# First token tile and mask constants moved from GpSimd's load queue to ScalarE's and SyncE's

## What is computed

```python
mod = silu(c) @ w_ada + b_ada                # 6 x 1024, split in shift1, scale1, gate1, shift2, scale2, gate2
h = rms_norm(x) * (1 + scale1) + shift1
q, f, i, g, B, C, hv = split(h @ w_in)       # 7 blocks of 512 columns
# HGRN2 recurrence over q, f, i with output gate g; short convolution over B, C, hv
x = x + gate1 * (concat[o_hgrn, o_conv] @ w_out)
x = x + gate2 * (relu(rms_norm2(x) @ w_up)**2 @ w_down)
y = rms_norm(x) * g_final
```

## Time and profile before

| what | value |
|---|---|
| three runs | 895.25, 898.47, 898.91 us |
| profiled execution, its own time | 894.26 us |
| its span, slowest core (core 0) | 892.7 us |
| spans of the eight cores | 883.8 to 892.7 us |
| PE busy | 825.2 us, 92% of the span |
| DVE, ACT, POOL busy | 482.7, 361.1, 173.4 us |
| GpSimd's queue (q0) | 44.14 MB written, 29.6% of the 16 DMA engines' time |
| SyncE's queue (q1), ScalarE's (q10) | 55.46 and 6.03 MB, 18.3% and 2.1% |

### The profile page before, as it was taken

The page is one execution under the profiler, slowest core; times in us unless marked ns, Lnnn a source line. Parts: engine busy times, 40 slices in busy tenths (PEclk is TensorE's granted clock), DMA queues, the critical chain, the costliest instruction groups (busy, mean ns, idle before and its releaser), DMA issues.

```text
span 892.7 us, 16990 instructions; the slowest of 8 cores (883.8 to 892.7 us)
## 1 busy us (share of the span) xinstructions
PE 825.2 (92%) x6005; PEld 521.0 (58%) x6005; DVE 482.7 (54%) x902; ACT 361.1 (40%) x771; POOL 173.4 (19%) x231
## 2 busy tenths in 40 slices
PE   1488899999999999876999999999999999999996
PEld 1356687677775776734544654465456545654864
DVE  1365797577777867771551764256335634542422
ACT  3266874546667666612401532233123312311412
POOL 3110134344115235200002101100210111011002
PEclk9888999999999999989999999999999999999999
DMA  8999914958995243999993513122222113102001
GB/s 154 193 193 195 200 45 98 193 171 173 205 206 139 96 142 72 189 167 173 187 210 109 194 52 115 48 95 71 95 84 71 60 48 118 36 13 89 30 2 48
DMA packets 27727, 106.71 MB, mean 120 GB/s; under 512 B 3798, under 2 KB 4822, under 8 KB 22652
## 3 DMA queue, kind: packets, MB, share of 16 engines
q0 software_dynamic: 6624, 44.14, 29.6%
q1 hardware_dynamic: 19292, 55.46, 18.3%
q10 hardware_dynamic: 1728, 6.03, 2.1%
HBM read 123.93 MB, written 22.68 MB: 164 GB/s over the span
## 4 chain that ended last, share of the span: by engine, by line
PE 81%; DMA 7%; issue 4%; DVE 4%; ACT 3%; POOL 0%; DVEq 0%; ACTq 0%; POOLq 0%; SPq 0%
PE B L484 79%; DMA xn<-x 4%; DMA xe<-xp 3%; PE B L495 2%; ACT W L511 2%; DVE W L522 1%; DMA cB<-constB 0%; DVE W L518 0%; DVE Sd L518 0%; DVE W L528 0%; ACT A L511 0%; DVE mix L518 0%; DVE hT L524 0%; DVE W L532 0%; ACT WX L511 0%
## 5 line engine op out<-in xcount | busy, mean ns | idle before, releaser
L484 PE MATMUL B<-h2T,wup 128*128 128x384 bf16 (+1 forms) x1536 | 242.2, 319 | 9.0 <-DVE uT L518 6.9
L484 PE MATMUL B<-wdn,uT 128*128 128x512 bf16 (+1 forms) x1120 | 237.5, 373 | 0.0
L511 ACT ACTIVATE W<-B 128x384 f32<-128x384 f32 (+2 forms) x241 | 119.0, 496 | 231.7 <-PE B L484 206.6
L484 PEld LDWEIGHTS B<-h2T,wup 128*128 128x128 bf16 x1536 | 150.2, 98 | 95.5 <-issue 12.2
L484 PE MATMUL B<-hT,win 128*128 128x256 bf16 (+1 forms) x1728 | 199.8, 273 | 6.5 <-DMA win<-w_in 4.8
L484 PEld LDWEIGHTS B<-hT,win 128*128 128x128 bf16 x1728 | 162.1, 100 | 32.3 <-issue 7.3
L484 PEld LDWEIGHTS B<-wdn,uT 128*128 128x128 bf16 x1120 | 109.0, 98 | 121.9
L518 DVE TENSOR_TENSOR uT<-W,B 128x384 bf16<-128x384 f32 (+1 forms) x192 | 100.5, 530 | 108.8 <-ACT W L511 87.8
L518 POOL TENSOR_TENSOR xr<-xr,W 128x512 f32<-128x512 f32 x63 | 82.6, 1312 | 284.4 <-DVE W L518 264.1
L518 DVE TENSOR_TENSOR W<-B,Gp 128x512 f32<-128x512 f32 (+1 forms) x65 | 44.0, 679 | 106.2 <-PE B L484 103.5
L484 PE MATMUL B<-wout,mix 128*128 128x512 bf16 x272 | 64.9, 390 | 9.1 <-DVE mix L518 7.0
(11 more groups left out here) (150 smaller groups left out, 643.7 us busy)
## 6 DMA issues: line engine op xcount, KB each, us to landing
x<-xr SPq DMA_DIRECT2D x17, 512.0 KB, 5.9
xn<-x SPq DMA_DIRECT2D x17, 512.0 KB, 4.4
xr<-x SPq DMA_DIRECT2D x17, 512.0 KB, 3.4
ada<-w_ada POOLq DMA_DIRECT2D x8, 1024.0 KB, 16.4
xr<-xp SPq DMA_DIRECT2D x16, 512.0 KB, 7.6
wdn<-w_down POOLq DMA_DIRECT2D x8, 1024.0 KB, 35.3
wup<-w_up POOLq DMA_DIRECT2D x8, 1024.0 KB, 22.3
yp<-xr SPq DMA_DIRECT2D x15, 512.0 KB, 2.6
```

Of the source, the lines that this page charges most:

```text
L484: ins = e.matmul(o_, lhsT=l_, rhs=r_, start=st, stop=sp_, skip_group_check=True)
L511: return P.op("act", lambda e: e.activation(out=out, in_=in_, func=func, **kw), r, w, c, prio=prio)
```

## The change

The two blocks of tile 0 are loaded on ScalarE's and SyncE's queues, the first entry of each. The mask constants are loaded as float32 behind the first block on ScalarE's queue, into the work tile `WX0`, and VectorE casts them into `cB`. The second block stands ahead of `cin`, `cF` and `vecT` on SyncE's queue. `load_first(0)` is gone, so the first load of GpSimd's queue is `ada2`.

```diff
     P.buf("cBm", P.bufs["cB"].rng, "cB")
+    x0 = [xnR.take(), xnR.take()]
+    dma("act", x0[0][0][:], xp_d[0:128, :], [], [x0[0][1]], 128 * 4096)
+    dma("sp", x0[1][0][:], xp_d[128:256, :], [], [x0[1][1]], 128 * 4096)
+    cf_, cfn = wall[9]
+    dma("act", cf_[:, 0:NCD], cB_d[:, :], [], [cfn], 128 * 4 * NCD)
     dma("sp", cin[:].rearrange("p k n -> p (k n)"), cc_d[:, :], [], ["cin"], 128 * 544)
-    dma("pool", cB[:, 0:NCD], cB_d[:, :], [], ["cB"], 128 * 4 * NCD)
     dma("sp", cF[:], cF_d[:, :], [], ["cF"], 128 * 4 * NCF)
     dma("sp", vecT[:], vec_d[:, :], [], ["vecT"], 128 * 288)
+    copy("dve", cB[:, 0:NCD], cf_[:, 0:NCD], [cfn], ["cB"])
     memset("pool", cB[:, CO:CO + 128], 1.0, ["cBm"])
...
-    xs_first = {}
+    xs_first = {0: x0}
...
-    load_first(0)
     load_ada(2); load_ada(3)
     load_in(1)
     load_first(1)
```

## The result

The changed kernel is slightly slower. The ratio of its time to that of the kernel before is 1.0052, with a 95% interval of 1.0028 to 1.0077: 4.7 us on 898.1, between 2.5 and 6.9. The same two kernels, timed again on another chip at the end of the study, gave 1.0025 (1.0004 to 1.0045), which is 2.3 us. Both intervals lie above 1, so the sign is sure; the two estimates of the size, 2.3 and 4.7 us, are about at the 0.5% that a measurement can tell from no change.

What follows compares the result with a forecast made beforehand. The start was taken to hang on GpSimd's load order up to the second A (41.74). The stream's 2.5 us gain goes unused, since late `vecT` delays that A: +1.5 us on 898.47 gives 900.0 us, range 894 to 905.5.

Steps and rivals of the forecast that it cites:

- lead of 2.5 us: GpSimd's load stream: input block 1, `xe` and all behind them land 2.5 us sooner, bounds 0 to 3.0.
- the wait for `vecT`: TensorE at the start: `vecT` delays `hT` of tile 0, so the second A starts at 43.25, +1.5 us.
- Turns on SyncE's queue: SyncE's small loads: each piece waits for one weight piece, 0.75 us a turn, so `vecT` lands at about 31.
- low bound of 26: `vecT` on SyncE's queue lands at 26 if weights come late and tile 0 passes at full speed; sum then -2.5.
- rival 1: SyncE's small loads don't queue behind weights, leaving the `xe` chain its 2.5 us gain: 896.0; chance 0.17.
- the prediction's own sign: At TensorE's first projection: the step on its order is wrong if A of tile 0 doesn't wait for `vecT`.
- nT ready by 22: Start of tile 0: `cB` lands near 18, VectorE casts it, and tile 0 is transposed by 22, costing nothing.
- 15% rule: The planner's load model, expected to have `vecT` usable near 30 and `xe` near 31.
- Rival 3: The planner reorders steps in the mixer; three waits, 7.7 us together, double or vanish: 892 or 906; chance 0.14.
- Rival 2: TensorE's wait for `hT` of tile 0: `vecT` later still, at 34.8, costing +5.3 us, 903.8; chance 0.19.
- The rest: `cin`, `cB` and its cast, GpSimd's memsets and ScalarE's two issues: all end before `vecT` or cost nothing.

Runs made afterwards that it cites:

- the experiment with 90%: The changed kernel, with its planner giving the plain queues 90% of the bandwidth in its first 6 us in place of 15%; ratio 1.0048 to the kernel before.

## Why the prediction was right, and where its reasons were wrong

The forecast was 1.5 us slower, counted as no change, with a range of 894.0 to 905.5. Measured is 4.7 us, or 2.3 in the repeat; 1.0052 of 898.47 is 903.1, inside the range. The direction and the place, the start up to the second A, were right. The mechanism was mostly wrong, and that the time came out near was in good part luck. A lead of 2.5 us that wasn't there was set aside as not used; the wait for `vecT`, which made the 1.5, wasn't the wait; and two things were left out: the order of the steps, which put the second A 4.3 us later (mean of the cores), and TensorE's clock, by which 1.6 of them came back.

**GpSimd's stream, 2.5 us sooner: there is no lead.** `xe` was used at 31.44 and not at 28.5, `ada3` at 24.17 and not at 21.4. The step that failed is the reading of the earlier trace rows: the slow flow from 2 to 5 us was taken for idle room that the small `cB` wasted. The stretch that the earlier trace rows leave out shows the DMA engines 94% busy in the middle of it:

```profile
3.00:4.00 1.00, 0.00 (x0) 0.00 (x0) 0.00 (x0) 1.00 (x1) 1.00 (x3) 1.00 0.94 45
```

The experiments with the constants alone and with the scale blocks first show that GpSimd's queue is slow there without `cB` too (1.25 and 2.2 us for a piece). With the change it got nothing until 6 us, while tile 0 filled the engines; that this cost it time shows in the 3.4 us by which the first scale block comes sooner without tile 0 there. The plain queues did use the time: from 2 to 6 us the engines moved 0.78 MB, before 0.47. But from 6 to 10 us they moved 0.80 MB, before 0.99, and the constants are now 192 KB where the cast load wrote 96. The lower bound of this term, 0, was about the value: `ada2` is used 0.2 us sooner than before, `ada3` 0.3 and `xe` 0.4 later.

**Turns on SyncE's queue: the price was right, their number was not.** From `cin` to `cF` it took 7.2 us, from `cF` to `vecT` 6.65, for 9 turns each: 0.80 and 0.74 a turn where 0.75 was forecast from the earlier trace rows. The packets bear the turns out: from 12 to 20 us the trace counts 171 of GpSimd's queue and 172 of SyncE's, one for one, and for the store of the earlier trace rows, from 388.0 to 412.7 us before, 522 and 525. But `cin` landed at 10.4 and not at 17.7. Tile 0 and most of `cin` passed before the weights filled the engines (six packets of GpSimd's queue up to 8 us), which is the same late start of GpSimd's stream as in the first term. So `vecT` came at 24.25, below the low bound of 26. The Trainium skill, "DMA: Bandwidth & Descriptors", section "Queues, rings and completion order", has an engine drain some 9 to 17 descriptors of one ring before it turns; a load of 9 pieces would then take one turn. The trace disagrees again: such a load took 6.65 us, a piece for each weight piece. So rival 1 was right that part of the small loads pass ahead of the weights, and wrong that none queues.

**TensorE waits for `vecT`: it waited for the order.** This is the step that made the forecast, and it failed by the prediction's own sign: A of tile 0 did not wait for `vecT`. It was forecast at 35.85 because `vecT` is late, and came at 38.10, the second A at 47.06 and not 43.25. The likeness of the first number is chance. "nT ready by 22" failed: its second half was copied at 32.50. The sum took over the order of the kernel before (A of tile 0, then the transposes of tile 1) while saying that the planner has `vecT` usable near 30. By the planner's 15% rule tile 0 became usable at 20 to 24 us, the constants that its transposes need at 28 and `vecT` near 30, about when `xe` did; it interleaved the two tiles. That its guess of the loads did it is shown by the experiment with 90%, which brought tile 0's order back. On the chip tile 0 was there at 9.2. With the order put right by hand and `vecT` equally late, the ratio is 1.0003: the term "the second A waits for `vecT`" is worth nothing that can be measured, and the order is worth the loss at the start, 2.2 to 2.7 us of the stage's start.

**Rival 3 named the cause at the wrong place.** It had the planner turn steps around, at a chance of 0.14, but looked for it in the mixer after 60 us. There the order did change: TensorE's wait for `kt` fell from 2.2 to 0.4 us on core 0, and its wait for `h2T` at the start of the MLP rose from 2.3 to 3.6 us (mean of the cores, in the repeats too). But the time from the next stage to the MLP stayed at 339.8 us. Its price of up to 7.7 us was more than the start lost. **Rival 2** failed: `vecT` wasn't later than 31.

**The rest cost nothing**, as forecast: the cast of `cB` took 0.36 us, and GpSimd's memsets delayed no load that TensorE waited for. (A load there waits for the one six places ahead of it, not five: `ada1`, the seventh, was issued at 17.94, after `ada2`.)

What stays open: the first comparison lost 4.7 us where the stage starts 2.7 later. The first two profiles differ in one later place, by more than the shift at 53 us, which by the prediction would mean the planner's order. The part of the MLP from the first product with `w_up` to the first with `w_down` took 49.7 us before and 54.0 after (mean of the six undisturbed cores), and TensorE's wait for `uT` of VectorE in it 4.9 and 7.9. The repeats, on two chips, have 52.0 and 53.2 there, and 6.5 and 6.6 us of that wait. The kernel with the order put right has 53.4 and lost nothing. So most of that difference is the first profile of the kernel before, which was quick there, and not the change; whether a microsecond of it is the change is not shown. The repeat has 2.3 us for both the time and the stage, and its interval overlaps the first one, so the surplus may be scatter. Nor do the runs show why GpSimd's queue brings little before 5 us, only that it does so with tokens or weights at its head, or what an early `vecT` in the right order would bring.

## What to carry to other kernels

In a kernel whose order is planned from a model, a moved load changes the order of the steps too: compare the lists of each engine before costing the move, and correct the model's landing times where a trace has the real ones. A low transfer rate at the start of a queue is not room that another load could use until a run shows it. Beside GpSimd's stream of weights the last load on SyncE's queue was late whatever its size (36 KB landed at 24.25 us, 512 KB was used at 23.06, 10 KB at 24.62), so the load that goes last must be one that no early step needs, nor one that stands ahead of such a step in an engine's list.

## What was not expected of the hardware

GpSimd's queue was slow before about 5 us with tokens (1.25 us for a piece of 4 KB) and with weights (2.2 us for a piece of 8 KB) at its head, in part beside small loads of the other queues, though 0.73 us a piece is what two weight blocks need in the stream. The plain queues could use that time: 307 GB/s from 4 to 5 us. And a load of 10 KB (`cF`) took as long as one of 36 KB (`vecT`) beside the weights, 7.2 and 6.65 us. Both have 128 rows, and beside the weights the pieces of SyncE's queue passed one for one with those of GpSimd's (172 and 171 from 12 to 20 us).
